# Rope tables and bank reads moved ahead, memory heads one group behind the other, and a begin with memory rows first and x turned inside a product

## The reference

```
mk, mv = split(mem @ w_mem_kv)                  # 4 memory heads of 64
h = layer_norm(x)
for i in 0..3:                                  # layers a0, b0, c0, a1
    proj = h @ w_in[i]
    a: branch = real part of a 2D Fourier transform of h
    b: branch = attention, 16 query heads on 4 key heads, rms norm of q and k, axial rope
    c: branch = three dilated attentions of 16 heads each with rope, mixed by their log sums
    gate, qm = tail of proj
    mem_out = softmax(qm mk^T / 8) mv
    h = layer_norm(8^0.25 h + (concat(branch, mem_out) * silu(gate)) @ w_out[i])
for l in 0..1:                                  # second block, not touched by the change
    three mixers (gated spatial, state space, latent attention), then a squared relu MLP
out = rmsnorm(x)
```

## Time and profile before

| | |
|---|---|
| median of 3 runs | 1325.59 us (1324.34 to 1328.61) |
| the profiled execution's own time | 1323.54 us |
| its span, first to last instruction | 1321.7 us |
| TensorE busy | 1255.1 us, 95% |
| VectorE busy | 873.1 us, 66% |
| ScalarE busy | 704.4 us, 53% |
| DMA engines | 46% of their time, 149 GB/s |
| mean granted TensorE clock | 0.993 |

### The profile page before, as it was taken

How to read it: one execution, slowest core, us unless ns; L and a number is a source line. 1 busy time by engine, 2 the same in 40 slices (tenths; PEclk the granted TensorE clock), 3 DMA queues, 4 the chain that set the end, 5 groups by cost and what they waited for, 6 DMA issues and landing times.

```text
span 1321.7 us, 20000 instructions
## 1 busy us (share of the span) xinstructions
PE 1255.1 (95%) x7972; PEld 1100.0 (83%) x7972; DVE 873.1 (66%) x1574; ACT 704.4 (53%) x1025; POOL 2.4 (0%) x8
## 2 busy tenths in 40 slices
PE   5999998999999999998898999999999999999997
PEld 5897777778888787887797997989898987989895
DVE  6566996586574756546566897665646897765545
ACT  4634577453457656565524676544444576544442
POOL 0000000000000000000000000000000000000000
PEclk9999999999999999999999999999999999999999
DMA  9335432445543434234332554456563544556560
GB/s 300 111 113 167 152 113 80 160 135 196 180 159 108 148 127 160 96 100 132 113 114 90 168 169 127 148 172 223 161 218 120 150 157 128 160 166 217 178 220 32
DMA packets 146914, 197.28 MB, mean 149 GB/s; under 512 B 4716, under 2 KB 102278, under 8 KB 146694
## 3 DMA queue, kind: packets, MB, share of 16 engines
q1 hardware_dynamic: 146694, 195.96, 45.6%
q0 software_dynamic: 128, 0.04, 0.0%
HBM read 194.94 MB, written 1.05 MB: 148 GB/s over the span
## 4 chain that ended last, share of the span: by engine, by line
PE 75%; DVE 14%; ACT 6%; issue 4%; DMA 1%; SPq 0%; ACTq 0%; DVEq 0%
PE bank L474 21%; PE bank L476 21%; PE bank L475 21%; PE bank L562 4%; DVE w_lo L2110 4%; DVE stat L2130 2%; ACT w_hi L1560 1%; PE bank L1053 1%; PE bank L1090 1%; PE bank L675 1%; PE bank L766 1%; DVE arena L2124 1%; DVE stat L2127 1%; PE bank L915 1%; DMA arena<-in_mem 1%
## 5 line engine op out<-in xcount | busy, mean ns | idle before, releaser
L2110 DVE TENSOR_TENSOR w_lo<-w_raw,w_hi 128x2048 fp32r<-128x2048 f32 (+5 forms) x190 | 413.5, 2183 | 130.9 <-ACT w_hi L1560 128.2
L1560 ACT ACTIVATE w_hi<-w_raw 128x2048 fp32r<-128x2048 f32 (+5 forms) x190 | 346.2, 1828 | 282.7 <-PE bank L476 272.5
L474 PE MATMUL bank<-h_hi,w_hi 128*128 128x256 f32 x976 | 279.2, 286 | 6.6 <-DVE w_lo L2110 3.4
L475 PE MATMUL bank<-h_lo,w_hi 128*128 128x256 f32 x976 | 276.0, 283 | 0.0
L476 PE MATMUL bank<-h_hi,w_lo 128*128 128x256 f32 x976 | 276.0, 283 | 0.0
L474 PE MATMUL bank<-w_hi,r_hi 128*128 128x512 f32 (+3 forms) x536 | 207.3, 387 | 2.3 <-DVE r_lo L2806 2.1
L475 PE MATMUL bank<-w_lo,r_hi 128*128 128x512 f32 (+3 forms) x536 | 204.1, 381 | 0.0
L476 PE MATMUL bank<-w_hi,r_lo 128*128 128x512 f32 (+3 forms) x536 | 204.0, 381 | 0.0
L474 PEld LDWEIGHTS bank<-h_hi,w_hi 128*128 128x128 f32 x976 | 187.0, 192 | 12.6 <-issue 8.2
L475 PEld LDWEIGHTS bank<-h_lo,w_hi 128*128 128x128 f32 x976 | 187.1, 192 | 0.5
L476 PEld LDWEIGHTS bank<-h_hi,w_lo 128*128 128x128 f32 x976 | 187.0, 192 | 0.0
(11 more groups left out here) (289 smaller groups left out, 1367.6 us busy)
## 6 DMA issues: line engine op xcount, KB each, us to landing
w_raw<-in_mlp_w SPq DMA_DIRECT2D x64, 1024.0 KB, 5.4
w_raw<-in_w_out SPq DMA_DIRECT2D x24, 1024.0 KB, 5.0
w_raw<-in_w_in_c SPq DMA_DIRECT2D x48, 512.0 KB, 4.4
w_raw<-in_w_in_c SPq DMA_DIRECT2D x18, 1024.0 KB, 4.9
w_raw<-in_w_in_a SPq DMA_DIRECT2D x12, 1024.0 KB, 5.9
w_raw<-in_w_in_b SPq DMA_DIRECT2D x12, 1024.0 KB, 5.1
w_raw<-in_w_in SPq DMA_DIRECT2D x8, 1024.0 KB, 5.2
w_raw<-in_w_out SPq DMA_DIRECT2D x8, 512.0 KB, 3.7
```

What stands on the lines that cost most here:

```text
L474: nc.tensor.matmul(o, lhs[0], rhs[0], start=start, stop=False)
L475: nc.tensor.matmul(o, lhs[0], rhs[1], start=False, stop=False)
L1560: nc.scalar.activation(w_hi[:, u % SPLIT_SLOTS, 0:kts * n], w_raw[:, u % RAW_SLOTS, 0:kts * n], ACT.Copy).then_inc(w_rounded.sem, w_rounde ...
L2110: v.tensor_tensor(w_lo[:, s, 0:m], w_raw[:, u % RAW_SLOTS, 0:m], w_hi[:, s, 0:m].bitcast(F32), ALU.subtract)\
```

## The change

1. **Begin.** The memory rows are issued ahead of unit 0. TensorE makes 14 products of the identity with itself (128 columns) before the memory rows, and 6 products of 512 columns behind the turned gain columns; both go to bank 3 and are never read. ScalarE makes the memory tiles' high parts before it rounds unit 0. x is turned between the two token halves of the memory values. VectorE splits unit 1 between the statistics of the second half of x and its norm, and unit 2 ahead of the tiles. The turned tiles 0 and 2 are scaled by VectorE, 1 and 3 by ScalarE, each in its own place instead of two shared ones.
2. **Loads.** The kept tables are split: the first part stays where it was, the rope tables and all behind them are issued after unit 6, under a semaphore of their own. The 14 small loads are issued after unit 4.
3. **Rope gains** of layer b are made in a0, after the weights of gate 0.
4. **Memory heads** of the a layers: the first pair is scaled right after its exponentials, before the second pair's maxima; ScalarE copies the first pair's turned tiles before the second pair's exponentials; TensorE makes gate 1 ahead of the second pair's turning, and `tokens(2)` behind it ahead of the second pair's values. The outputs are gated in the order 0, 1, 4, 2, 3.
5. **Layers b and c:** part 0 of `heads_out` stands ahead of the next `pair_max`.
6. **Layer c:** the first 18 projection parts rotate over banks 0, 1, 2, 4, 5; gate 2 is in bank 1.

The core of the diff:

```diff
+            for _ in range(14):
+                nc.tensor.matmul(bank[3][:, 0:P], ident, ident, start=True, stop=True)
             pe.wait_ge(mem_loaded, 16)
...
+            for _ in range(6):
+                nc.tensor.matmul(bank[3][:, :], ident, mem_in[:, 0, 0:512], start=True, stop=True)
...
             feature_major(("mem", "k"), 4, rows_of(A["w_mem_kv"], 0, KT, 0, MEM_W), rT)
-            hidden_from_rows("in", 0)
...
                     i = mm3(o[:, b * MEM_W:(b + 1) * MEM_W], rT(k, b), [a[:, k, :] for a in w], k == 0, k == KT - 1)
+                if b == 0:
+                    hidden_from_rows("in", 0)
```

```diff
+        C_EARLY_BANKS = (0, 1, 2, 4, 5)
...
-                    C_BANK[(*section, n, b)] = len(C_BANK) % 3
+                    C_BANK[(*section, n, b)] = C_EARLY_BANKS[len(C_BANK) % 5] if len(C_BANK) < 18 else len(C_BANK) % 3
```

TensorE and ScalarE in an a layer:

```diff
                     pair_values(0)
+                    gate_product(1)
                     pair_turned(1)
-                    gate_product(1)
+                    tokens(2)
                     pair_values(1)
-                    tokens(2)
                     gate_product(2)
...
                     pair_exp(0)
                     sines(0)
+                    pair_turned(0)
                     pair_exp(1)
                     gate_silu(0)
-                    pair_turned(0)
                     sines(1)
+                    gate_silu(1)
                     pair_turned(1)
-                    gate_silu(1)
```

SyncE's queue, and ScalarE's begin:

```diff
+            sp.dma_start(mem_in, A["mem"][0].rearrange("(b p) d -> p b d", p=P)).then_inc(mem_loaded, 16)
             load_unit(0)
-            sp.dma_start(mem_in, A["mem"][0].rearrange("(b p) d -> p b d", p=P)).then_inc(mem_loaded, 16)
...
-            sp.dma_start(const[:, P:], A["const"][:, P:n_kept]).then_inc(consts_loaded, 16)
+            late = CONST_AT["axial_cos"][0]
+            sp.dma_start(const[:, P:late], A["const"][:, P:late]).then_inc(consts_loaded, 16)
...
                 load_unit(u)
+                if u == RAW_SLOTS + 1:
...
+                if u == 2 * RAW_SLOTS:
+                    sp.dma_start(const[:, late:], A["const"][:, late:n_kept]).then_inc(tables_loaded, 16)
...
-            round_unit(0)
             for j in range(4):
                 act.wait_ge(product_done.sem, product_done.at(("mem", "t", j)))
                 nc.scalar.activation(flat2(r_hi[:, 2 * j:2 * j + 2, :]), bank[4 + j][:, :], ACT.Copy).then_inc(split_hi.sem, split_hi.next(("mem", j)))
+            round_unit(0)
+            evac(("cols", "a"), col_a[:], bank[0][:, 0:N_COL_A], ahead=0)
             round_unit(1)
-            evac(("cols", "a"), col_a[:], bank[0][:, 0:N_COL_A])
```

VectorE in the heads of layer c (layer b has the same with `heads_out(q - 3, ...)`), and its tail:

```diff
+                            out = {5: (0, (L, "ao", 0)), 9: (1, (L, "ao", 1)), 11: (4, (L, "mo"))}.get(q)
+                            if out:
+                                heads_out(*out, (0,))
                             if q:
                                 pair_max(q)
                             weights((L, "s", q, 1), SPLIT_SLOTS)
                             if q:
                                 pair_recip(q)
...
+                            if out:
+                                heads_out(*out, (1, 2))
...
                     for q in range(C_TAIL, C_TAIL + 4):
+                        if q == C_TAIL + 1:
+                            heads_out(2, (L, "ao", 2), (0,))
                         pair_max(q)
                         pair_recip(q)
                         if q == C_TAIL + 1:
-                            heads_out(2, (L, "ao", 2))
+                            heads_out(2, (L, "ao", 2), (1, 2))
```

More of the change, by code:

```diff
@@ L572, in hidden_from_rows @@
                                 pe.wait_ge(*left[b0 + j])
-                            left[b0 + j] = tiles_read.after((L, "zt", j))
+                            left[b0 + j] = (tiles_scaled if j % 2 else tiles_read).after((L, "zt", j))
                         elif j < 2:
@@ L826, in _ @@
                     gate_product(3)
-                    for of in (4, 0, 1, 2, 3):
+                    for of in (0, 1, 4, 2, 3):
                         r_ready.at((L, of))
@@ L1134, in _ @@
                     qk_section(3)
-                    feature_major((L, "gate", 2), 2, rows_of(w, 0, KT, 3 * DIL_W + 2 * 256, 256), hT, reader=gate_read)
+                    feature_major((L, "gate", 2), 1, rows_of(w, 0, KT, 3 * DIL_W + 2 * 256, 256), hT, reader=gate_read)
                     turn(3, 2)
@@ L1645, in _ @@
                                      scale=S_(8 + b, 1), bias=S_(10 + b, 1)).then_inc(rows_normal.sem, rows_normal.next(("in", b, n)))
-            hidden_hi("in", "a0", split_t, tiles_read)
+            evac(("mem", "k"), flat2(mkT[:, :, :]), bank[4][:, :], ahead=0)
+            round_unit(3)
+            gain, shift = ln_cols(0)
+            for j, what in ((1, "scaled"), (0, "hi"), (1, "hi"), (3, "scaled"), (2, "hi"), (3, "hi")):
+                if what == "scaled":
+                    act.wait_ge(product_done.sem, product_done.at(("in", "zt", j)))
+                    for m in range(2):
+                        k, half = 2 * j + m, slice(m * S, (m + 1) * S)
+                        ins = nc.scalar.activation(tile_place(j)[:, half], bank[j][:, half], ACT.Identity, scale=gain[:, k:k + 1], bias=shift[:, k:k + 1])
+                    ins.then_inc(tiles_scaled.sem, tiles_scaled.next(("in", "zt", j)))
+                else:
+                    there = tiles_scaled if j % 2 else tiles_read
+                    act.wait_ge(there.sem, there.at(("in", "zt", j)))
+                    nc.scalar.activation(flat2(h_hi[:, 2 * j:2 * j + 2, :]), tile_place(j), ACT.Copy).then_inc(h_rounded.sem, h_rounded.next(("a0", j)))
+            evac(("mem", "v"), flat2(mv[:, :, :]), bank[5][:, :], ahead=0)
             act.wait_ge(ident_loaded, 16)
@@ L1883, in _ @@
                     act.wait_ge(product_done.sem, product_done.at((L, "gate", 2)))
-                    nc.scalar.activation(flat2(gate[:, 4:6, :]), bank[2][:, :], ACT.Silu).then_inc(gate_read.sem, gate_read.next((L, "gate", 2)))
+                    nc.scalar.activation(flat2(gate[:, 4:6, :]), bank[1][:, :], ACT.Silu).then_inc(gate_read.sem, gate_read.next((L, "gate", 2)))
                     turn(3, 2)
@@ new lines, in first_tiles @@
+            def first_tiles():
+                gain, shift = ln_cols(0)
+                for j in (0, 2):
+                    product(("in", "zt", j), 1)
+                    for m in range(2):
+                        k, half = 2 * j + m, slice(m * S, (m + 1) * S)
+                        ins = v.tensor_scalar(tile_place(j)[:, half], bank[j][:, half], gain[:, k:k + 1], shift[:, k:k + 1], MUL, ADD)
+                    ins.then_inc(tiles_read.sem, tiles_read.next(("in", "zt", j)))
+                for j in range(4):
+                    pair = slice(2 * j, 2 * j + 2)
+                    there = tiles_scaled if j % 2 else tiles_read
+                    dve.wait_ge(there.sem, there.at(("in", "zt", j)))
+                    dve.wait_ge(h_rounded.sem, h_rounded.at(("a0", j)))
+                    v.tensor_tensor(flat2(h_lo[:, pair, :]), tile_place(j), flat2(h_hi[:, pair, :]).bitcast(F32), SUB).then_inc(h_ready.sem, h_ready.next(("a0", j)))
@@ L2321, in _ @@
                                 .then_inc(row_max.sem, row_max.next((L, q, par)))
-                    for q in range(2):
                         dve.wait_ge(scores_read.sem, scores_read.at((L, "s", q, 1)))
@@ L2410, in pair_normal, with heads_out @@
                             ins.then_inc(probs_normal.sem, probs_normal.next((L, q, par)))
-                    def heads_out(q):
+                    def heads_out(q, parts=range(3)):
                         if q > 1:
@@ L2439, in _ @@
                         pair_normal(q - 1)
+                        if q % 2 == 0:
+                            heads_out(q - 3, (0,))
                         pair_max(q)
@@ L2503, in pair_recip, with heads_out @@
                             v.reciprocal(S_(52 + 2 * sl, n), S_(32 + 4 * sl, n)).then_inc(row_recip.sem, row_recip.next((L, q, par)))
-                    def heads_out(j, key):
+                    def heads_out(j, key, parts=range(3)):
                         weights(key, 0 if j == 3 else SPLIT_SLOTS - 1)
@@ L2510, in heads_out @@
                             dve.wait_ge(gate_ready.sem, gate_ready.at((L, "late" if j == 3 else "early")))
-                        gated(L, j, key, bank[C_OUT_BANK][:, :], ahead=0 if j == 3 else SPLIT_SLOTS - 1)
+                        gated(L, j, key, bank[C_OUT_BANK][:, :], parts, ahead=0 if j == 3 else SPLIT_SLOTS - 1)
                     def heads(*at):
```

101 lines of the change are left out of this document (41 added, 60 removed).

## The result

The changed kernel takes 1317.33 us (median of 5 runs, 1316.74 to 1317.47) against 1324.64 (5 runs, 1322.98 to 1328.61): ratio 0.9943, 95% interval 0.9932 to 0.9954, 7.3 us less. Measured once more later beside the experiments it took 1315.69 (1314.70 to 1316.82) against 1324.35 (9 runs, 1323.64 to 1326.45), ratio 0.9928, 0.9916 to 0.9941. The forecast was 1315, the range 1307 to 1321.

What follows compares the result with a forecast made beforehand. TensorE is busy 95% of the span, so only its pauses and half-clock stretches can be won. Begin 3.0, memory heads 3.1, layer b 0.25 + 2.9 and layer c 1.2 sum to 10.5 us: 1315, range 1307 to 1321.

Steps and rivals of the forecast that it cites:

- the heads of a0 and a1: Memory heads: early scaling of the first pair gains 0.8 + 2.3 = 3.1 us, despite two new waits of 1.7 each.
- the rope tables: Layer b: making them in a0 removes a 1.02 us pause, but VectorE's chain leaves a gain of 0.25.
- gate 2's bank and the pause at 439: Layer c: bank 1 removes gate 2's 1.36 us pause wholly; the 0.80 pause at 439.02 gives 0.3.
- the loss in layer c's tail: Pair 15's turning comes later because its maxima stand behind a weight split: the 1.55 pause goes, net 0.6 us lost.
- Layer b's bank read: heads_out part 0 before the next maxima removes pauses of 1.50 at 203.29 and 231.51; gain 2.9 us.
- the sign named for it: Layer b: no 1.50 pauses, and a pause near 2 where 1.30 was; 0.2 comes back in VectorE's order.
- Rival A: New waits do not bite and all named pauses go: 10 us more gain, 1305; chance 0.12.
- The term that was mis-sized is the begin's 3.0: Begin: earlier memory keys at full clock and earlier weights let the first query product end at 36.9, not 39.9: 3.0 us.
- The prediction's own mark of being wrong: Begin: the prediction is wrong if the turned tiles of x come later than the values' end.
- Rival B: Memory heads: the clock falls in four pauses of 1.7, costing 6.8 us, leaving 3.7: 1322; chance 0.08.
- Rivals C and D: Begin: C, clock rises at 15.4, 1317, inside the forecast's 0.66; D, half clock until queries are done, 1336, 0.05.
- Rival E: Begin or heads give only what they take (longer VectorE chain, load behind 14 small ones): 1322 to 1325; chance 0.09.

Runs made afterwards that it cites:

- e8: Changed kernel with layer b's first heads_out part taken behind the present pair's maxima again, as in the kernel before; 1317.72 us.
- e3: Changed kernel with the a layers' memory heads reordered: ScalarE's pair-1 exponentials before pair-0 copies, pair-1 turning before gate 1 and its silu; 1309.02 us.
- e5: The changed kernel once more, unchanged, as the reference of the experiments; 1315.69 us.
- e6: Changed kernel without the 14 small unread products of the begin, the 6 wide ones kept; 1314.61 us.
- e11: Changed kernel with only ScalarE's pair-1 exponentials moved ahead of its pair-0 copies in the a layers' memory heads; 1313.10 us.
- e2: Changed kernel without the 14 small and 6 wide unread products of the begin; 1314.69 us.
- e1: Changed kernel with ScalarE's rounding of weight unit 3 moved from ahead of the tile scaling to behind the split of h_hi 3; 1313.55 us.
- e4: Changed kernel with the edits of e1 and e3, and layer c's first output of chunk 2 asking weights one ahead, not two; 1306.26 us.
- e7: e4 without the 14 small unread products of the begin; 1306.38 us.
- e9: Changed kernel with layer c's early products rotating over three banks again instead of five, gate 2 keeping its new bank; 1315.52 us.
- e10: Changed kernel with the ten small rope-table instructions moved back from a0 to the start of layer b; 1315.71 us.

## Why the prediction was right or wrong

**Right in place and nearly in size:** the heads of a0 and a1 (-0.71 and -2.23 for -0.8 and -2.3), whose two new waits came out at 1.74 and 1.82. Here luck helped: the forecast took the lengths before, 24.15 and 25.65, with the half clock in them, and none for the time after. The clock did stay up in the result, and in all such pauses of the other profiles but one (e8), but how often the kernel before falls there, its one profile can't tell. Also right were the rope tables (0.3 for 0.25); gate 2's bank and the pause at 439 (1.36 and 0.80, forecast 1.7 together, found 1.81 with the rest of that stage); and the loss in layer c's tail (+0.43 for +0.6, pause 1.65). Layer b's bank read was 3.3 to 3.4 by e8 for 2.9; the sign named for it, a pause near 2 where 1.30 was, did not come (1.32 at 165.73), so the 0.2 that the sum gave back was not given back. Rival A, in which no new wait bites, is out: the new waits of 1.74, 1.82, 1.49 and 1.65 stand in the trace.

**The term that was mis-sized is the begin's 3.0.** Its measured size is 1.0 to 2.1, and -0.3 in the profile of the result. The step that failed is the one that let ScalarE scale its tiles from 28.8. The steps before it came out (keys 15.93 for 16.2, values 22.99 for 23.3, x turned at 25.97 for 26.3). I had unit 3 rounded before 28.8; in fact ScalarE began it at 28.65 in that profile, at 27.76 to 28.82 in e3, e5, e6 and e8 to e11, and at 26.14 in e2 alone, and ended 1.92 later. The prediction's own mark of being wrong, that the turned tiles of x come later than the values' end, was there: the values had ended, and TensorE waited 2.19 us for h_lo. I priced the DMA issues that were moved (the tables and 14 small loads, which now come later) but took unit 3's landing as early enough without a row for it, and did not ask what a late landing would hold up on ScalarE's queue. e1 shows it, with e4 and e7: with the same transfer behind the tiles, the begin gives 3.2 to 4.2. The issue could have been had from the prediction's own sum: it has the first weights split at 16.0, and unit 3's transfer waits for that split (issued at 15.89).

**Rival B, half clock in the new pauses, did not come, though its mechanism is real.** It asked for all four pauses of 1.7. In the result's profile none of these four dropped the clock; the unforeseen one of 2.19 did. Over the profiles, the pause of 1.65 at pair 15's turning dropped it in e2, e9 and e10 and in seven others not; that of 1.74 in a0 in e8 and in seven others not. One fall costs 1.5 to 1.6. The Trainium skill (TensorE: Matmul & The Clock Gate, HAM oscillation) has gaps re-throttle the engine; the traces agree that they can, and show that a gap of 1.65 or 1.74 us mostly does not.

**Rivals C and D** are out: the lengths of the small products and the end of their batch, at 9.13 here and 7.8 to 9.1 in others (8.6 forecast), put the rise well before 10. C's 1317 is met in number only. **Rival E** named the right kind of fault (the begin gives back what it took, by a load) with the wrong load: behind it was a weight unit, not the 14 small ones.

**Half clock in the stages not touched** went with 1.6 us more in the profiled pair. I had no term for that. In a1's spectral stage it changes between executions of nearly the same program; in the second block the loss of 0.7 to 1.2 stands in all twelve profiles with the change. The median moved by 7.3 and the second time by 8.7, both nearer to the forecast's 10.5 than the 6.1 of the profiled pair.

## What to carry to other kernels

For a step that moves ahead, write down for every instruction in the same engine's queue behind it when its own input lands: here a rounding that waited for its weights until 28.65 stood ahead of tiles that were ready at 27.9. The begin won 3.2 to 4.2 us with it behind them; with it ahead, and the unit late, it won 1.0 to 2.1, and nothing where the clock fell at 32 as well. Compare stages before and after with the clock beside them: both kernels' heads had about the same pauses, and the difference was half clock behind two of them. A removed pause is worth its length only if what follows did not wait for the same chain: 1.12 for a bank was worth 0.0, 1.02 for a weight 0.3, 1.50 for a bank read 1.7. When a pause is named with its releaser, changing the order of calls on the releasing engine is the cheapest trial: such edits in three places (the begin, the a layers' heads, layer c's tail) gave 9.4 us, more than the whole change (8.7 by its second measurement).

## What the runs showed of the hardware

- A fall to half clock behind a pause is not a fixed price: pauses of 1.65 and 1.74 us dropped the granted clock in some executions (3 of 10 and, in a0, 1 of 8) and left it at 1.00 in others, with the same instructions around them. Those of 1.86 (e6), 1.95 (e11) and 2.03 (e5) left it up; of the two of 2.11 in the kernel before (the earlier trace rows and the same in a1) only the first was followed by half clock; those of 2.13 (e9), 2.19 (after), 2.45 (before, a1) and 2.61 (e10) were followed by half clock. Where the same stage can be compared, a fall cost 1.5 us (tail of c, 34.5 for 33.0) to 1.6 (heads of a0 in e8). Behind pauses of 3.4 to 3.7 us it fell in every profile (0.54 or 0.77 over 6.9 us).
- TensorE can start a stage with the clock low at next to no cost: in e2 the memory keys ran at half clock for 4.8 us, and the values began at 22.62, no later than in the changed kernel (22.99), since their weights were split only at 22.24.
- The same unit's transfer lands at different times: ScalarE began to round unit 3 at 26.14 to 28.82 us in the nine profiles in which that rounding stands ahead of the tiles.
- The two medians of the same changed kernel differ by 1.6 us (1317.33 and 1315.69), those of the kernel before by 0.3; single differences under 2 us in this document rest on stage lengths, not on medians.
